# Expert matrices loaded as halves, at most three on their way

## What is computed

```
group = top-1 of 8 groups;  two experts of the 8 in that group, with weights
hid   = silu(x @ w1[e]) * (x @ w3[e])        # w1, w3: 1024 x 512
y     = hid @ w2[e]                          # w2: 512 x 1024
out   = sum over a token's two experts of gate * y
```

## Time and profile before

| what | us |
|---|---|
| median of 3 runs | 3673.42 |
| lowest, highest | 3670.94, 3673.61 |
| the profiled execution | 3671.4 |
| its span in the profile | 3669.6 |
| PE, PEld busy | 2984.2 (81%), 1559.9 (43%) |
| DVE, ACT, POOL busy | 673.6 (18%), 489.9 (13%), 254.9 (7%) |
| moved, all queues | 587.39 MB, mean 160 GB/s |

### The profile page before, as it was taken

One profiled execution on the slowest core, in us unless ns is written; L12 is line 12 of the kernel. 1 busy time (PEld: TensorE's weight loads), 2 busy tenths in 40 slices (PEclk: granted clock), 3 DMA queues, 4 the chain that ended last, 5 costly groups with the idle time before them and its releaser, 6 DMA issues. The chain is left out here.

```text
span 3669.6 us, 29297 instructions
## 1 busy us (share of the span) xinstructions
PE 2984.2 (81%) x12116; PEld 1559.9 (43%) x12116; DVE 673.6 (18%) x1777; ACT 489.9 (13%) x954; POOL 254.9 (7%) x247
## 2 busy tenths in 40 slices
PE   6999999999865455454455449999999999999999
PEld 4666666544642122122122126444444464444443
DVE  1222222210130000100100032332220123321102
ACT  1222232210010000000000021310000113110000
POOL 1000002210000000000000030020000110110000
PEclk9999999999977777787777679899999998999999
DMA  6211111112179998898889841112221211122220
GB/s 199 52 35 52 35 35 52 46 46 92 55 302 428 379 381 345 378 393 358 378 365 393 355 174 71 58 46 69 80 92 69 71 60 68 41 74 80 78 83 35
DMA packets 192664, 587.39 MB, mean 160 GB/s; under 512 B 16434, under 2 KB 142642, under 8 KB 167730
## 3 DMA queue, kind: packets, MB, share of 16 engines
q1 hardware_dynamic: 186210, 569.19, 40.3%
q10 hardware_dynamic: 4160, 8.39, 0.6%
q0 software_dynamic: 2192, 8.39, 0.6%
HBM read 571.26 MB, written 14.68 MB: 160 GB/s over the span
## 5 line engine op out<-in xcount | busy, mean ns | idle before, releaser
L2310 PE MATMUL bank<-arena 128*128 128x512 f32 (+2 forms) x1472 | 608.9, 576 | 9.1 <-DVE arena L1675 9.1
L1068 PE MATMUL bank<-arena 128*32 128x512 f32 x2048 | 264.5, 674 | 224.2 <-DMA arena<-in_moe_w 223.1
L330 PE MATMUL bank<-arena 128*128 128x384 f32 x1280 | 430.9, 489 | 14.3 <-DMA arena<-in_w_in 14.3
L2310 PEld LDWEIGHTS bank<-arena 128*128 128x128 f32 x1472 | 276.0, 191 | 340.1 <-issue 330.1
L330 PEld LDWEIGHTS bank<-arena 128*128 128x128 f32 x1280 | 237.4, 190 | 175.1 <-DMA arena<-in_w_in 14.5
L2319 PE MATMUL bank<-arena 128*128 128x512 f32 x704 | 303.2, 592 | 0.0
L1077 PE MATMUL bank<-arena 128*128 128x128 f32 x128 | 28.8, 366 | 280.6 <-DVE arena L1319 280.6
L1790 PE MATMUL bank<-arena 128*128 128x512 f32 (+3 forms) x736 | 250.2, 498 | 0.0
L1068 PEld LDWEIGHTS bank<-arena 128*32 128x32 f32 x2048 | 75.4, 122 | 411.0 <-issue 411.0
L2319 PEld LDWEIGHTS bank<-arena 128*128 128x128 f32 x704 | 133.1, 189 | 168.4 <-issue 168.4
L1790 PEld LDWEIGHTS bank<-arena 128*128 128x128 f32 x736 | 138.3, 190 | 101.2 <-issue 69.5
(11 more groups left out here) (299 smaller groups left out, 2571.7 us busy)
## 6 DMA issues: line engine op xcount, KB each, us to landing
arena<-in_moe_w SPq DMA_DIRECT2D x192, 2048.0 KB, 24.4
arena<-in_w_up SPq DMA_DIRECT2D x44, 1024.0 KB, 7.7
arena<-in_w_in SPq DMA_DIRECT2D x52, 512.0 KB, 5.7
arena<-in_w_down SPq DMA_DIRECT2D x10, 2048.0 KB, 7.7
arena<-in_w_in SPq DMA_DIRECT2D x12, 1024.0 KB, 5.2
y_slots<-arena ACTq DMA_DIRECT2D x32, 256.0 KB
arena<-in_w_in SPq DMA_DIRECT2D x4, 2048.0 KB, 9.5
arena<-in_w_out SPq DMA_DIRECT2D x4, 2048.0 KB, 8.2
```

What stands on the lines that cost most here:

```text
L330: ins = pe.matmul(banks[s % 2][:, 0:CW], m.aT[:, k, tile(t)], w[:, k, :], start=(k == 0), stop=(k == KT - 1))
L1068: ins = pe.matmul(banks[pr][q:q + CAP, :], m.xt[:, k, c:c + CAP], up_view(m, slots[2 * e2 + up])[:, k, :], start=(k == 0), stop=(k == KT - 1))
L2310: ins = pe.matmul(banks[2 * (j % 2) + half][:, part], w[:, k, c0:c0 + P], m.aT[:, k, part], start=(k == 0), stop=(k == KT - 1))
```

## The change

Each matrix is loaded by two DMAs, one for each half of every partition's 16 KB (8 KB each): for w1 and w3 that is steps k = 0..3 and 4..7 of the up product, for w2 steps f = 0, 1 and 2, 3. TensorE raises a new semaphore `up_half` after step k = 3 of the up product. SP's loop is written out, with constant positions: for every two positions it loads both first halves and then both second halves. A first half waits for `up_half` of the pair that used the slot, a second for `up_done` (both for `down_done` for w2), and each load also waits until the matrix three positions before has landed whole (`UNDERWAY`). The first eight matrices are loaded as halves too, in the norm block, without waits. TensorE waits for 32 in a slot's semaphore instead of 16. `Need` leaves out a wait that an earlier one of the same engine covers.

```diff
+UNDERWAY = 3
...
-def load_expert(sp, m, G, A, at, i):
-
-    pp, j = at // 6, at % 6
-    e = 8 * i + 2 * pp + (j // 2 if j < 4 else j - 4)
-    sp.dma_start(m.w[at % WSLOT], expert_src(A, PARTS[j], e)).then_inc(G[f"e_in{at % WSLOT}"], 16)
+def load_half(sp, m, G, A, at, h):
+
+    pair, j = at // 6, at % 6
+    e = 2 * pair + (j // 2 if j < 4 else j - 4)
+    half = slice(KT * FF // 2 * h, KT * FF // 2 * (h + 1))
+    sp.dma_start(m.w[at % WSLOT][:, half], expert_src(A, PARTS[j], e)[:, half])\
+      .then_inc(G[f"e_in{at % WSLOT}"], 16)
...
     for at in range(WSLOT):
-        load_expert(sp, m, G, A, at, 0)
+        for h in range(2):
+            load_half(sp, m, G, A, at, h)
...
-    def loads(i, n):
-        for x in range(n):
-            pp, j = x // 6, x % 6
-            sp.wait_ge(G["up_done" if j < 4 else "down_done"], 4 * i + pp + 1)
-            load_expert(sp, m, G, A, x + WSLOT, i)
-
-    with sp.Fori(0, NIT - 1) as i:
-        loads(i, 24)
-    loads(NIT - 1, 24 - WSLOT)
+    need = Need(sp)
+    for two in range(WSLOT, NLOAD, 2):
+        for h in range(2):
+            for at in (two, two + 1):
+                pair, j = (at - WSLOT) // 6, (at - WSLOT) % 6
+                need(G[("up_half", "up_done")[h] if j < 4 else "down_done"], pair + 1)
+
+                landed = at - UNDERWAY
+                need(G[f"e_in{landed % WSLOT}"], 32 * (landed // WSLOT + 1))
+                load_half(sp, m, G, A, at, h)
...
         for j in range(4):
-            pe.wait_ge(G[f"e_in{slots[j]}"], 48 * i + 16 * ((6 * pp + j) // WSLOT) + 16)
+            pe.wait_ge(G[f"e_in{slots[j]}"], 96 * i + 32 * ((6 * pp + j) // WSLOT) + 32)
...
+            if k == KT // 2 - 1:
+                ins.then_inc(G["up_half"], 1)
         ins.then_inc(G["up_done"], 1)
...
         for j in range(4, 6):
-            pe.wait_ge(G[f"e_in{slots[j]}"], 48 * i + 16 * ((6 * pp + j) // WSLOT) + 16)
+            pe.wait_ge(G[f"e_in{slots[j]}"], 96 * i + 32 * ((6 * pp + j) // WSLOT) + 32)
```

More of the change, by code:

```diff
@@ L913 @@
 WSLOT = 8
+UNDERWAY = 3
 ROUTER_SEMS = ["rw_in", "logits_done", "logits_ready", "r_exp_in", "r_exp", "assigned", "counted",
                "routed", "zeroed", "eb_sent", "eb_in", "r_step"]
-MOE_SEMS = ["up_done", "hs_ready", "hid_ready", "ht_turned", "ht_ready", "down_done", "yo_ready",
+MOE_SEMS = ["up_done", "up_half", "hs_ready", "hid_ready", "ht_turned", "ht_ready", "down_done", "yo_ready",
             "y_sent0", "y_sent1", "g_ready", "gather_done", "xt_ready", "g_step",
```

## The result

| | before | after |
|---|---|---|
| median, us | 3672.18 (4 runs) | 3718.36 (4 runs) |
| lowest, highest | 3670.17, 3673.61 | 3717.62, 3720.51 |
| span in the profile | 3669.6 | 3716.5 |

A forecast was written before the change was run, and what follows sets the result against it. Two store-carrying DMA engines, full from first refill to last, were taken to bound the experts' stage. Packets +6, start -3.5, end +5 summed to +7.5, say +7 on 3671.4: 3678 us, +5 against the median; range 3667 to 3702.

The forecast's parts named there:

- halves, packet price: Weight loads: two 8 KB packets take 0.617 us, 0.004 more than one of 16 KB; +6 us, bounds 0 to +40.
- stores ahead, and the end: Stage's end: store work ahead of the last weight +13, last down product starting earlier -6.5; together +5 us (0 to +6.5).
- earlier room, at the start: First pair's up product: first refill released after half of 7.09 us; -3.5 us (0 to -4).
- the limit of three: SP's loads, each waiting for the matrix three back: the two full engines never run dry, so 0 us.
- prompt stores: Stores take 25 us instead of 44, no longer pile up; VectorE's 753 us of waiting mostly go; no time gained mid-stage.
- the worthlessness of earlier room in the middle: Middle of the experts' stage: the limit, not room, ends last, so early release is worth nothing there.
- 4 per 11.4 us, hidden too: SP's loop: 368 loads of about 0.44 us each to issue, four per 11.4 us, claimed to cost no time.
- Covered: 0: Limit: at a landing the two full engines hold 4.9 us of packets, next bytes take 1.3 us; cost 0.
- Rival C: SP's wait for the matrix three back starves the pair, from 4.9 us landing to bytes; 5.5 us gives +55; 8%.
- rival B: Weight loads: smaller packets or alternating halves cost more, +15 to +40 us, from 0.620 us per two packets; 10%.
- The line: Packet times: straight line from 2 KB in 0.080 us and 16 KB in 0.613 gives 0.308 us for 8 KB.
- rival E: Loads: each DMA pays its own latency, 3.0 us on each of 184 more, +552 us, 4223; 1%.

The follow-up runs named there:

- c6: The kernel before with stores spread over sixteen engines (c1) and each load of the loop as two half-matrix DMAs back to back: 3554.45 us.
- c1: The kernel before with each store cut in two DMAs of 64 partitions, spreading stores over all sixteen engines: 3541.30 us.
- b2: The kernel before with each load of the loop as two half-matrix DMAs; first eight whole, no limit, no early release, stores on two engines: 3689.22 us.
- a2: The kernel after with its first eight matrices loaded whole and the limit at eight matrices under way instead of three: 3684.74 us.
- a5: a2 with the first halves' room also given back only at the end of the up product: 3689.53 us.
- a1: The kernel after with its first eight matrices loaded as whole DMAs of 2 MB: 3700.71 us.
- b4: The kernel before with whole matrices, SP's loop written out and at most three matrices on their way: 3706.52 us.
- c4: b4 (whole matrices, written-out loop, limit of three) with the stores spread over sixteen engines: 3540.06 us.
- d1: The kernel before with its first eight matrices as twelve DMAs, matrices 0 to 3 as halves and four whole: 3680.22 us.

## Why the prediction was wrong

By its own steps, the change's 46 us, each from the runs. The sum closes in part by construction, since most rows are steps from one kernel to the next; medians repeat within 1 or 2 us, so the two rows under 5 us are good to that much only.

| step | predicted | measured | from |
|---|---|---|---|
| halves, packet price | +6 (0 to 40) | +13.2 | c6 less c1 |
| stores ahead, and the end | +5 (0 to 6.5) | +3.6 | b2, less the row above |
| earlier room, at the start | -3.5 (0 to -4) | -4.8 | a2 less a5 |
| the limit of three | 0 | +16.0 | a1 less a2 |
| first eight as sixteen DMAs | no term | +17.7 | after less a1 |
| sum | +7.5 | +45.7 | after: +46.2 |

**What bounds the kernel** was read rightly: two engines carry the stores and are full; c1 is the proof and gave the size of it. So were the prompt stores, the worthlessness of earlier room in the middle, and the last pair.

**The missing term** is the sentence that wasn't there. The prediction's loop counted SP's issues "4 per 11.4 us, hidden too" for the 368 loads in the block and said nothing on the sixteen ahead of it. They were in the diff. The rows of before show eight issues in 4 us and no hold, so no row gave the price of a held queue; but a doubled burst of issues on an engine that all others must meet at the block's end deserved a bound, by the transfer time of what is issued: up to 40 us.

**The step that failed in its reasoning** is "Covered: 0" for the limit. It asked only whether the two full engines run dry, and took their packets to last as long as before. The limit hardly starves them: in the kernel after fewer than two engines are busy for some 1 to 2 us of the stage in all. It ties the *fourteen others* to the two's landings, so that they stop and start more than twice as often as without it, and packets around these stops are slower, those of the two engines among them. Rival C named the limit as the place and 4.9 us as the deciding number; place right, mechanism not, since b4 has 9.8 us in hand and pays more. That the two's packets are slower is shown by their records in b4 (32 of 34 us), and that it takes lagging engines by c4. In the kernel after the same sum, 1472 x 2 x 3.1 ns = 9 us of the 16, leaves some 7 us open; it takes the packets behind a store for all, and a third of the two's weight packets follow none. That the stops cause the slowness, and how, is argued from c4 and from where the slow packets lie.

**The packet price** had the right form in rival B (it decides from 0.620 us on for two packets; c6 gives 0.622 by 0.613 + 0.009) and was mis-sized by half. The line was drawn through two rates counted in short windows, where one packet more or less on each engine (of 54 in the earlier trace rows) is 2%, 11 ns, so its fixed part of 4 ns was below what the rows could tell; it also left out that halves double the DMAs and their completions. The runs don't separate packet and completion. The forecast's chances (38% slower) held the sign at its second largest; the range missed since it had no room for two such terms at once.

The Trainium skill's fixed 2 us per DMA (page DMA: Bandwidth & Descriptors, section Anatomy of one DMA, where it is fitted to DMAs issued by GpSimd; these come from SP), rival E, is not what happens behind a filled queue: c6 has 184 more DMAs and pays 0.07 us for each.

## What to carry to other kernels

Where one DMA engine of the sixteen lags, look for a small transfer whose outermost dimension is small: the share of engines busy while it runs alone (2/16 here) told it; here stores with 2% of the stage's bytes cost 131 us. A limit on transfers under way was free while the engines kept one pace (c4) and cost 16 and 34 us where they didn't (a1, b4). Cutting transfers in parts has a price per further packet (9 ns, the same for halves and quarters), and a price in the issuing queue that only a burst meets: count the DMAs outstanding, ahead of a block's end above all.

## What the hardware showed that was not expected

- SP is held at a DMA's issue with about ten outstanding, whatever their size: 0.5 us an issue until then, 2.1 us after (kernel after: sixteen halves in 16.9 us; d1: held from the eleventh; eight of 2 MB: never).
- Packets are slower where other engines stop and start: 16 KB packets average 0.614 us on the two engines before, 0.636 in b4; over all engines a busy engine moves 3.6% less in a1 than in a2, with the same packets.
- TensorE after 3.3 us of idling (d1) had 0.50 of its clock, 1.2 GHz, for all 13.9 us of the router's 64 products of 72 columns, busy throughout; after 1.0 us of idling it ran them at 1.00 (kernel before, a1). So 2.3 us of lateness cost 8.9.
